# Layer-norm statistics taken apart and issued earlier, and the PSUM evacuations of two projection stages moved to VectorE

## What is computed

```python
h = _modulate(x, sh1, sc1)            # layernorm(x) * (1 + sc1) + sh1
proj = h @ w_in
u_ssm = proj[..., :SSM_WIDTH]         # SSM_WIDTH = 1024, D_MODEL = 2048
y_a = _s5_branch(u_ssm, ...)          # state-space scan over the sequence
...
merged = sigmoid(g_a) * y_a + sigmoid(g_b) * y_b
x = layernorm(ALPHA * x + g1 * (merged @ w_out), ln1_g, ln1_b)
x = layernorm(ALPHA * x + g2 * sq_relu_mlp(modulate(x, sh2, sc2)), ln2_g, ln2_b)
```

## Time and profile before

| | before |
|---|---|
| timed, two runs: median | 3209.96 us |
| timed, lowest and highest | 3160.24 and 3259.69 us |
| profiled execution, its own time | 2993.21 us |
| its span (slowest core, core 0) | 2991.4 us |
| spans of the 8 cores | 2955.1 to 2991.4 us |
| mean granted TensorE clock by core | 0.801 to 0.804 |
| TensorE matmul busy | 1852.1 us (62%) |
| VectorE busy | 1083.7 us (36%) |
| ScalarE busy | 380.2 us (13%) |

### The profile page before, as it was taken

How to read it: one execution, slowest core, us unless ns; L and a number is a source line. 1 busy time by engine, 2 the same in 40 slices (tenths; PEclk the granted TensorE clock), 3 DMA queues, 4 the chain that set the end, 5 groups by cost and what they waited for, 6 DMA issues and landing times.

```text
span 2991.4 us, 25637 instructions; the slowest of 8 cores (2955.1 to 2991.4 us)
## 1 busy us (share of the span) xinstructions
PE 1852.1 (62%) x9192; PEld 883.2 (30%) x9192; DVE 1083.7 (36%) x1815; ACT 380.2 (13%) x661; POOL 143.7 (5%) x109
## 2 busy tenths in 40 slices
PE   2302253155121364686878849569999999999950
PEld 1101121022111122343433424224444444444420
DVE  2488344544554242121212113634421321321343
ACT  0011121012111111011111100331001001001001
POOL 0000000000000000000000000000000000000013
PEclk8655586578555676798989979779999999999975
DMA  8900610020000415777777663655445545544512
GB/s 122 143 5 1 127 43 0 7 93 15 0 0 0 64 24 77 96 99 103 103 102 103 96 169 57 120 91 85 77 64 84 83 64 80 85 66 76 85 56 84
DMA packets 199210, 213.20 MB, mean 71 GB/s; under 512 B 3384, under 2 KB 192304, under 8 KB 194352
## 3 DMA queue, kind: packets, MB, share of 16 engines
q0 software_dynamic: 186896, 164.11, 37.2%
q1 hardware_dynamic: 12192, 47.47, 5.5%
HBM read 367.28 MB, written 8.39 MB: 126 GB/s over the span
## 4 chain that ended last, share of the span: by engine, by line
PE 57%; DVE 19%; DMA 14%; issue 4%; ACT 4%; POOL 1%; DVEq 1%; SPq 0%; ACTq 0%; POOLq 0%
PE bank L1047 45%; DMA s_BIG<-w_ada 6%; PE bank L710 5%; DMA s_wb<-w_ada 3%; DVE s_BIG L825 2%; DVE s_stat L659 2%; DMA s_wb<-w_in 2%; PE bank L1075 2%; PE bank L957 2%; DMA s_wb<-w_out 1%; PE bank L416 1%; POOL s_BIG L1287 1%; DVE s_HT L684 1%; DMA s_wb<-w_glu_gate 1%; DVE s_BIG L1288 1%
## 5 line engine op out<-in xcount | busy, mean ns | idle before, releaser
L1047 PE MATMUL bank<-s_HT,s_wb 128*128 128x512 bf16 x3072 | 670.1, 381 | 16.4 <-DMA s_wb<-w_ff 16.4
L1047 PE MATMUL bank<-s_wb,s_RB 128*128 128x512 bf16 x2560 | 555.2, 380 | 47.9 <-DMA s_wb<-w_out 42.2
L1047 PEld LDWEIGHTS bank<-s_HT,s_wb 128*128 128x128 bf16 x3072 | 302.1, 98 | 381.7 <-issue 23.7
L1047 PEld LDWEIGHTS bank<-s_wb,s_RB 128*128 128x128 bf16 x2560 | 250.6, 98 | 352.3 <-issue 52.4
L710 PE MATMUL bank<-s_wb,s_HT 128*128 128x512 bf16 x512 | 143.3, 449 | 117.1 <-DVE s_HT L684 91.4
L1251 DVE TENSOR_TENSOR s_RB<-s_RB 128x512 bf16<-128x512 bf16 x128 | 54.2, 425 | 379.0 <-ACT s_RB L1249 379.0
L1047 PE MATMUL bank<-s_BIG,s_wb 128*128 128x512 bf16 x768 | 169.8, 383 | 22.3 <-DMA s_wb<-w_glu_gate 22.3
L1271 DVE TENSOR_TENSOR s_BIG<-bank,s_BIG 128x512 f32<-128x512 f32 x128 | 88.5, 692 | 250.1 <-PE bank L1047 250.0
L1249 ACT ACTIVATE s_RB<-bank 128x512 bf16<-128x512 f32 x128 | 76.4, 597 | 722.6 <-PE bank L1047 704.3
L1075 PE MATMUL bank<-s_BIG,s_crep 128*128 128x256 bf16 x384 | 61.8, 330 | 123.2 <-DMA s_BIG<-w_ada 123.2
L710 PEld LDWEIGHTS bank<-s_wb,s_HT 128*128 128x128 bf16 x512 | 55.9, 111 | 199.6 <-issue 160.8
(11 more groups left out here) (205 smaller groups left out, 1404.6 us busy)
## 6 DMA issues: line engine op xcount, KB each, us to landing
s_wb<-w_ff POOLq DMA_DIRECT2D x32, 2048.0 KB, 14.2
s_wb<-w_ada POOLq DMA_DIRECT2D x12, 2048.0 KB, 26.0
s_wb<-w_in POOLq DMA_DIRECT2D x12, 2048.0 KB, 23.7
s_BIG<-w_ada POOLq DMA_DIRECT2D x24, 1024.0 KB, 14.5
s_BIG<-x_own SPq DMA_DIRECT2D x16, 1024.0 KB, 7.4
s_BIG<-x_prev SPq DMA_DIRECT2D x8, 1024.0 KB, 5.9
s_wb<-w_out POOLq DMA_DIRECT2D x4, 2048.0 KB, 26.6
out<-s_BIG SPq DMA_DIRECT2D x8, 1024.0 KB, 3.9
```

The source lines that it names most:

```text
L1047: last = k.op("pe", lambda e, kc=kc: e.matmul(banks.f32(bk), lhsT=lhs_fn(kc), rhs=rhs_fn(kc), start=(kc == 0), stop=(kc == n_k - 1)), [fr_ ...
```

## The change

`ln_part` is cut in two. `ln_a(j)` holds the load of `xt`, the statistics, `bn_aggr` and the square root; `ln_b(j)` holds reciprocal, small product and normalisation. `transposes_to_hT` gets a flag `all_dve`, with which all 16 evacuations are on VectorE. `u_matmuls` is cut into `u_mm` (the 32 matmuls) and `u_ev` (two casts, both on VectorE). A step is now written in this order: transposes and evacuations of `j` (all on VectorE), tail copy, `ln_b(j+1)`, `ln_a(j+2)`, `u_mm(j)`, `u_ev(j)`. Both stages are rewritten so; the previous stage's edit is:

```diff
-                    if q % 2 == 0:
+                    if q % 2 == 0 and not all_dve:
...
+        def u_mm(hT_fn, j, deps):
+            res = []
+            last = None
+            for n2 in range(2):
+                bk, fr_ = banks.get()
+                for kc in range(16):
+                    last = k.op("pe", lambda e, kc=kc, bk=bk, n2=n2: e.matmul(banks.f32(bk), lhsT=hT_fn(kc), rhs=wu[n2][:, kc, :], start=(kc == 0), stop=(kc == 15)),
+                                [fr_] + list(deps) + wu_d[n2] if kc == 0 else (), signal=(kc == 15))
+                res.append((bk, last))
+            return res, last
+
+        def u_ev(Udst, j, res):
+            evs = []
+            for n2, (bk, last) in enumerate(res):
+                o = k.op("dve", lambda e, bk=bk, n2=n2: e.tensor_copy(out=Udst[:, 32 * n2:32 * n2 + 32, j, :], in_=banks.f32(bk).rearrange("p (g h) -> p g h", g=32)), [last])
+                banks.rel(bk, o)
+                evs.append(o)
+            return evs
+
+        def ln_a(xv, j, extra):
+            b2 = j % 2
+            d_x = k.dma("sp", xt[b2], xv[:, j, :], deps=[xt_free[b2]] + list(extra))
+            o = None
+            for q in range(4):
+                o = k.op("dve", lambda e, q=q, b2=b2: e.bn_stats(out=stat[:, q, :], in_=xt[b2][:, q * 512:(q + 1) * 512]), [d_x] if q == 0 else ())
+            o = k.op("dve", lambda e: e.bn_aggr(out=mv[:, j, :], in_=stat[:].rearrange("p a b -> p (a b)")), [o])
+            return k.op("act", lambda e: e.activation(out=sdv[:, j:j + 1], in_=mv[:, j, 1:2], func=AF.Sqrt, bias=EPS), [o])
+
+        def ln_b(j, o_sq):
...
+            xt_free[b2] = o_n
+            return o_n
...
-        o_ns = {0: ln_part(xpv, 0, [o_T[-1]])}
+        sq_ = {0: ln_a(xpv, 0, [o_T[-1]])}
+        o_ns = {0: ln_b(0, sq_[0])}
+        sq_[1] = ln_a(xpv, 1, [o_T[-1]])
         for j in range(8):
             b2 = j % 2
-            if j + 1 < 8:
-                o_ns[j + 1] = ln_part(xpv, j + 1, [o_T[-1]])
-            o_n = o_ns[j]
-            evs = transposes_to_hT(nbf[b2], lambda kc, b2=b2: hpT[b2][:, kc, :], sc1p, modA[:, 0, :], [o_n, hpT_free[b2], o_sc1p] + o_sh1)
+            evs = transposes_to_hT(nbf[b2], lambda kc, b2=b2: hpT[b2][:, kc, :], sc1p, modA[:, 0, :], [o_ns[j], hpT_free[b2], o_sc1p] + o_sh1, all_dve=True)
             nbf_free[b2] = k.last("pe")
             o_tl = k.op("act", lambda e, b2=b2, j=j: e.activation(out=tail[:, :, 2 * j:2 * j + 2], in_=hpT[b2][:, :, 126:128], func=AF.Copy), evs)
             tail_ops.append(o_tl)
-            ue, lastpe = u_matmuls(lambda kc, b2=b2: hpT[b2][:, kc, :], Uprev, j, evs)
+            if j + 1 < 8:
+                o_ns[j + 1] = ln_b(j + 1, sq_[j + 1])
+            if j + 2 < 8:
+                sq_[j + 2] = ln_a(xpv, j + 2, [o_T[-1]])
+            um, lastpe = u_mm(lambda kc, b2=b2: hpT[b2][:, kc, :], j, evs)
+            u_evs += u_ev(Uprev, j, um)
             hpT_free[b2] = [lastpe, o_tl]
-            u_evs += ue
```

More of the change, by code:

```diff
@@ L665, in ln_stats, with transposes_to_hT @@
             return o
-        def transposes_to_hT(nbf, dst_fn, scaleA, biasA, deps):
+        def transposes_to_hT(nbf, dst_fn, scaleA, biasA, deps, all_dve=False):
             evs = []
@@ L702, in build @@
             wu.append(buf); wu_d.append(dops); wu_i.append(bi)
+        def u_mm(hT_fn, j, deps):
[24 more added lines that the diff above has]
+        def ln_b(j, o_sq):
+            b2 = j % 2
+            o = k.op("dve", lambda e: e.reciprocal(out=rstd[:, j:j + 1], in_=sdv[:, j:j + 1]), [o_sq])
+            o = k.op("dve", lambda e: e.tensor_scalar(out=nmr[:, j:j + 1], in0=mv[:, j, 0:1], scalar1=rstd[:, j:j + 1], scalar2=-1.0,
+                                                     op0=ALU.mult, op1=ALU.mult), [o])
+            o_n = k.op("dve", lambda e, b2=b2: e.tensor_scalar(out=nbf[b2], in0=xt[b2], scalar1=rstd[:, j:j + 1], scalar2=nmr[:, j:j + 1],
+                                                            op0=ALU.mult, op1=ALU.add), [o, nbf_free[b2]])
+            xt_free[b2] = o_n
+            return o_n
         def u_matmuls(hT_fn, Udst, j, deps):
@@ L866, in build @@
         lastpe = None
-        o_ns = {0: ln_part(xov, 0, [])}
+        sq_ = {0: ln_a(xov, 0, [])}
+        o_ns = {0: ln_b(0, sq_[0])}
+        sq_[1] = ln_a(xov, 1, [])
         for j in range(8):
             b2 = j % 2
+            evs = transposes_to_hT(nbf[b2], lambda kc, j=j: HT[:, kc, j * 128:(j + 1) * 128], sc1p, modA[:, 0, :], [o_ns[j]], all_dve=True)
+            nbf_free[b2] = k.last("pe")
             if j + 1 < 8:
[L871 to L876, removed]
+                o_ns[j + 1] = ln_b(j + 1, sq_[j + 1])
+            if j + 2 < 8:
+                sq_[j + 2] = ln_a(xov, j + 2, [])
+            um, lastpe = u_mm(lambda kc, j=j: HT[:, kc, j * 128:(j + 1) * 128], j, evs)
+            u_evs += u_ev(U, j, um)
         for n2 in range(2):
```

## The result

| | before | changed |
|---|---|---|
| timed, median | 3089.3 us (10 runs) | 2969.4 us (11 runs) |
| lowest and highest | 2987.3 and 3274.4 us | 2958.1 and 3233.8 us |
| ratio, changed to before | | 0.9895, 95% interval 0.986 to 0.993 |
| profiled execution, own time | 2993.2 us | 2952.4 us |
| its span, slowest core | 2991.4 us | 2950.8 us |

The ratio is 31 us off 2991 us, with an interval of 21 to 42 us; the forecast was 30.8 us. By the 2% that was set as the bound, the kernel is neither faster nor slower. The forecast time of 3179 us was nevertheless 7% above the measured 2969 us, and the lower end of its range, 3100 us, 4% above it.

What follows compares the result with a forecast made beforehand. No engine bounds the whole; VectorE's path was taken to set most gaps in the two rewritten stages. Gaps -37.0 and +2.3, clock +3.9 give -30.8 us, so 3179 us from 3210, range 3100 to 3245.

Steps and rivals of the forecast that it cites:

- The level: Whole kernel: 31 us off the 3210 us median of two timed runs before, giving 3179 us.
- the clock rival: Bursts in both stages: clock stays up, 14 bursts take 7.18 us, -58.1 us in all, 3152 us (profile 2935); chance 0.10.
- Gaps into steps 1 to 6: Both stages, 12 gaps from cast to next matmul: 4.86 us instead of 7.94, 37.0 us less in all.
- rival of slower evacuations: VectorE's runs of 16 evacuations take 5.4 us, gap 6.2 us, only -12 us in all, 3198 us; chance 0.16.
- Gaps into step 7: One gap in each stage: evacuation on one engine makes it 4.86 us instead of 3.71, 2.3 us more together.
- Clock: Bursts after the gaps: clock falls each time; 12 keep 9.13 us, step 7's two go from 7.18 to 9.13, 3.9 us more.
- Work moved under the bursts: VectorE's normalisation, statistics and first cast, 5.5 us, fit under a burst of 9.13 us with 3.6 to spare; cost nothing.
- Loads: Loads of `x` in both stages: asked for about every 14.0 us, landing in 5.9 to 7.4 us; no cost.
- The late-load rival: VectorE waits for `x`; each us beyond 17.6 costs 1 us in 12 steps, at 25.5 us 3274 us; chance 0.05.
- Step 0: Start of both stages: previous stage unchanged, waiting for `w_in`; own stage 7.1 instead of 7.2 us on VectorE; nothing gained.
- The sum: All terms over both stages: -37.0 + 2.3 + 3.9 = -30.8 us, profiled execution from 2993.2 to 2962 us.

Runs made afterwards that it cites:

- 8 fillers: The changed kernel with 8 useless 512-column matmuls added between the transposes and matmuls of steps 1 to 7 in both stages; ratio to before 0.9881.

## Why the prediction was right or wrong

**The level: wrong.** The step that failed is "I take the same 31 us off: 3179 us". The saving was about right; the number it was taken from, the 3210 us median of two runs, was not the kernel's level. Later medians of the kernel before were 3089, 2993 and 2991 us, and in the first ten runs three lay between 2987 and 2995 us, where the profiled execution (2993.2) had been. The prediction had 2962 us in its hands, 0.25% from the 2969.4 us measured, and widened its range by the scatter of the two runs to both sides alike. But the times of this kernel don't lie around a middle: of 30 timed runs the shortest took 2987 us, 16 more lay within 0.5% of it, and the others reached up to 3274 us. A range should have reached from 2935 us (the clock rival on the profile's level) upward.

**Gaps into steps 1 to 6: right.** Forecast 3.08 us less each; measured 3.06 less, from 7.94 to 4.88 us, 16 evacuations in 4.12 us where 4.11 were forecast. The rival of slower evacuations is out.

**Gaps into step 7: right.** 3.71 and 3.68 us became 4.87 and 4.88, 2.4 us together for the 2.3 forecast.

**Clock: right in kind, off in size.** It fell in every step, as taken. But "the 12 bursts keep their 9.13 us" is a term that was mis-sized: from matmul start to cast they took 8.86 us in the previous stage and about 8.76 in the own stage, 3.9 us less in all. In the gap of the earlier trace rows the clock had fallen some 3 us before the burst, which then ran at half clock for some 4 us; now it falls about 1 us into the burst in the previous stage and at most 0.3 us before it in the own stage, where it is back after some 3.2 us. Step 7's two bursts grew by 3.3 us together instead of 3.9. The argument that carried this term, 4.07 us is nearer to 4.54 than to 2.93, was a poor one: the runs show falls after 2.36 us in every step, and after 2.90 us in 6 of 14.

**Work moved under the bursts: right,** free (VectorE waits 0.96 and 2.76 us inside the burst, 3.7 us to spare for the 3.6 forecast; the run with a cast less changed nothing). **Loads: right.** Apart from the first load of each stage, line 728 waits only once, 0.81 us in step 0 of the previous stage, under the wait for `w_in`. Even with a step of 8.11 us the loads of `x` don't delay TensorE. The late-load rival is out.

**Step 0:** nothing forecast, -0.6 us measured in all: the own stage is 1.4 us shorter there, 0.5 of it an earlier landing and 0.5 a shorter burst; the previous stage 0.8 us longer, its second half-burst having run longer at half clock (6.49 for 5.66 us in the earlier trace rows).

**The sum.** Measured in the two stages: 161.8 to 145.3 and 141.1 to 121.8 us (own stage forecast 15.4 us shorter, measured 19.3), 35.8 us for 30.8: the 5 us are the bursts (4.5) and step 0 (0.6). The profiled executions differ by 40.6 us. Of the rest, 3.8 us lie before the stages, where both kernels are alike (line 121's first load of `x` at 307.96 instead of 311.74), and 1.0 between and behind them. In nine of the ten profiled executions (all but that with the first cast on ScalarE) the part before the stages took 306 to 314 us and the part behind them 2251 to 2261 us, so these 4.8 us are what executions differ by. The ratio's 31 us with its interval of 21 to 42 covers 35.8; that it agrees with the forecast's 30.8 to the microsecond is luck.

## What to carry to other kernels

Look at what the waiting engine's releaser does between being ready and releasing: here two thirds of it was work for a later step, and moving that behind the release was worth over 2%, while giving the rest to one engine took about half of it back. Before moving work to balance engines, ask whether the engine it goes to stands on the path at that moment; busy shares (VectorE 36%, ScalarE 13%) say nothing about it. And take the level for a forecast in us from the lower edge of the runs and from the profiled execution, not from a median of two.

## What the runs showed of the hardware

The length of TensorE's wait does not decide alone whether the clock falls: it fell after 2.36 us of wait in 14 of 14 steps (8 fillers), after 2.90 us in 6 of 14, after 4.08 us in 14 of 14, never after 0.63 us. In these runs, where it fell, the next burst of 32 matmuls took 8.6 to 8.75 us instead of 7.07. It can also fall when the wait is already over: 0.6 us into the burst in the step shown with 8 fillers, about 1 us into it in the previous stage of the changed kernel. The Trainium skill (TensorE: Matmul & The Clock Gate, Why this matters for your kernels) asks that no idle gap between bursts be over about 3 us; the steps with 2.36 and 2.90 us show that staying under that did not keep the clock up here.
